# Gate projections of five feed-forward networks as seven block products instead of eight, each network in thirds

## The reference, cut to what matters

```python
def conv_ffn(n, w_up, conv_w, conv_b, w_down):
    u, g = jnp.split(n @ w_up, 2, axis=-1)
    gp = jnp.pad(g, ((0, 0), (pad, pad), (0, 0)))
    gc = sum(gp[:, j:j + S] * conv_w[j] for j in range(CONV_WIDTH)) + conv_b
    return (jax.nn.silu(gc) * u) @ w_down

def swiglu(x, w_gate, w_up, w_down):
    return (jax.nn.silu(x @ w_gate) * (x @ w_up)) @ w_down
```

## Time and profile before

| | us |
|---|---|
| median of 3 runs | 2785.27 (2784.6 to 2785.38) |
| span of the profiled execution | 2783.7 |
| PE busy | 2765.9 (99%) |
| DVE busy | 1427.2 (51%) |
| ACT busy | 1006.1 (36%) |
| POOL busy | 509.2 (18%) |

### The profile page before, as it was taken

The page is one execution under the profiler, slowest core; times in us unless marked ns, Lnnn a source line. Parts: engine busy times, 40 slices in busy tenths (PEclk is TensorE's granted clock), DMA queues, the critical chain, the costliest instruction groups (busy, mean ns, idle before and its releaser), DMA issues.

```text
span 2783.7 us, 33669 instructions
## 1 busy us (share of the span) xinstructions
PE 2765.9 (99%) x12836; PEld 2293.1 (82%) x12836; DVE 1427.2 (51%) x1392; ACT 1006.1 (36%) x1099; POOL 509.2 (18%) x364
## 2 busy tenths in 40 slices
PE   9999999999999999999999999999999999999999
PEld 7978889878888888888778888888888888888887
DVE  5778766566654444343575444334443455644422
ACT  4333633434432344332263444324443222344421
POOL 0124013041101310052123100121110222501100
PEclk9999999999999999999999999999999999999999
DMA  4212024223222322323212222232223322232232
GB/s 165 90 62 79 31 106 148 79 76 106 91 105 95 115 92 90 105 91 105 99 35 74 104 91 97 99 106 104 92 90 106 106 98 99 91 105 91 90 106 91
DMA packets 39676, 264.97 MB, mean 95 GB/s; under 512 B 4528, under 2 KB 5808, under 8 KB 8240
## 3 DMA queue, kind: packets, MB, share of 16 engines
q1 hardware_dynamic: 38016, 259.02, 26.8%
q10 hardware_dynamic: 1584, 4.87, 0.5%
HBM read 261.77 MB, written 2.10 MB: 95 GB/s over the span
## 4 chain that ended last, share of the span: by engine, by line
PE 96%; DVE 2%; ACT 1%; issue 0%; DMA 0%; SPq 0%; POOL 0%; DVEq 0%; POOLq 0%; ACTq 0%
PE ps L1793 30%; PE ps L1794 30%; PE ps L1795 30%; PE ps L1956 1%; PE ps L2022 1%; PE ps L2053 1%; PE ps L2347 1%; PE ps L2319 1%; PE ps L1978 1%; DVE w_lo L901 0%; PE ps L2036 0%; PE ps L2331 0%; ACT w_hi L450 0%; DMA stage<-in_stream 0%; PE ps L1833 0%
## 5 line engine op out<-in xcount | busy, mean ns | idle before, releaser
L450 ACT ACTIVATE w_hi<-stage 128x2048 fp32r<-128x2048 f32 x241 | 462.8, 1920 | 1354.3 <-PE ps L1795 1351.8
L1793 PE MATMUL ps<-x_hi,w_hi 128*128 128x512 f32 x2400 | 943.3, 393 | 2.2 <-DVE w_lo L977 2.0
L1795 PE MATMUL ps<-x_hi,w_lo 128*128 128x512 f32 x2400 | 934.0, 389 | 0.0
L1794 PE MATMUL ps<-x_lo,w_hi 128*128 128x512 f32 x2400 | 933.9, 389 | 0.0
L901 DVE TENSOR_TENSOR w_lo<-stage,w_hi 128x2048 fp32r<-128x2048 f32 x241 | 602.1, 2498 | 397.1 <-ACT w_hi L450 397.1
L1793 PEld LDWEIGHTS ps<-x_hi,w_hi 128*128 128x128 f32 x2400 | 450.6, 188 | 98.9 <-issue 3.5
L1794 PEld LDWEIGHTS ps<-x_lo,w_hi 128*128 128x128 f32 x2400 | 450.7, 188 | 95.4 <-issue 3.4
L1795 PEld LDWEIGHTS ps<-x_hi,w_lo 128*128 128x128 f32 x2400 | 450.5, 188 | 93.9
L1793 PE MATMUL ps<-f_hi,w_hi 128*128 128x512 f32 x880 | 342.7, 389 | 0.0
L1794 PE MATMUL ps<-f_lo,w_hi 128*128 128x512 f32 x880 | 342.3, 389 | 0.0
L1795 PE MATMUL ps<-f_hi,w_lo 128*128 128x512 f32 x880 | 342.3, 389 | 0.0
(11 more groups left out here) (401 smaller groups left out, 2616.3 us busy)
## 6 DMA issues: line engine op xcount, KB each, us to landing
stage<-in_stream SPq DMA_DIRECT2D x242, 1024.0 KB, 4.9
...
```

The costliest lines, as they stand in the source:

```text
L450: act.activation(w_hi[slot][:, :], stage[slot][:, :], ACT.Copy).then_inc(hi_ready, 1)
L1793: pe.matmul(out_ap, wh, xh, start=first, stop=False)
L1794: pe.matmul(out_ap, wh, xl, start=False, stop=False)
L1795: return pe.matmul(out_ap, wl, xh, start=False, stop=last)
```

## The change

Of a gate chunk's matrix A (1024 rows of input by 256 output columns) and the tokens B (1024 by 512), both are cut into halves each way: A into 512x128 blocks, B into 512x256. Eight block products make the two gate tiles; with sums of blocks on both sides seven do (Strassen's method, in the variant with 4 sums of weights and 4 of tokens). Each product is 4 row tiles, 3 matmuls each, of 256 columns.

- Rounds with seven products: 4 to 10 of FFN 0, 2 to 10 of the others (`SEVEN_FROM`). The rest stay at eight.
- DVE makes the four sums of weights from `stage` (`gate_sums`), ACT rounds them (`s_hi`), DVE subtracts (`s_lo`). Only three of the four blocks are also used singly, so the chunk's own split is 1536 wide.
- Once an FFN, ACT scales one quarter of `h` (`t_half`), DVE makes the four sums of tokens (`token_sums`, 16 instructions), ACT rounds and DVE subtracts (`token_lo`).
- DVE puts the products together: five steps while the chunk runs (`gate_early`; ACT first copies product 1 out of PSUM), two after it, and then two multiplications by `rstd` in SBUF (`gate_evac`).
- Each FFN is three parts of 4, 4 and 3 rounds, each followed by its share of down: four chunks, one for each pair of output tiles, of 8, 8 or 6 row tiles. The number of chunks stays 34 an FFN. DVE adds a share to `h` three times. `f_hi` and `f_lo` hold 8 tiles instead of 22, which frees the room for the sums.
- In FFN 1, `stat(3)`, its root and its reciprocal move to round 1, POOL's rescaling of `h` to rounds 1 to 3, and the first share of down waits for it.
- The FFNs are no loops any more: each step is written out on every engine.

Several semaphores were merged under new names elsewhere, with the same waits. The core of the diff:

```diff
+HALF = S // 2
+KP = KT // 2
+PARTS = [("a", 0, 4), ("b", 4, 4), ("c", 8, 3)]
+SEVEN_FROM = [4, 2, 2, 2, 2]
+NONE_OF = FT // 2
...
+f_hi = place("f_hi", HID, [P, 8, S], F32R)
+f_lo = place("f_lo", hid(8), [P, 8, S], F32R)
...
+s_hi = place("s_hi", hid(32), [P, 4 * KP * P], F32R)
+s_lo = place("s_lo", hid(36), [P, 4 * KP * P], F32R)
+s_f = place("s_f", hid(40), [P, 4 * KP * P])
+snap = place("snap", ROPE, [P, 3, HALF])
...
+S1, S3, S2, S4 = range(4)
+T1, T2, T3, T4 = range(4)
+SNAP_1, U2, U3 = range(3)
+PRODUCT = {1: (4, 0), 2: (4, 1), 6: (5, 0), 7: (6, 0), 5: (7, 0)}
+QUARTER = {(0, 0): 0, (1, 0): 1, (1, 1): 2, (0, 1): 3}
...
+T_GROUPS = {i: {0: [0, 1], 1: [2, 3]} if i == 0 else {0: [0, 1, 2, 3]} for i in range(5)}
+T_ROUND_AT = {i: 1 if i == 0 else 0 for i in range(5)}
...
+def gate_hi(i, it):
+    c, _ = gate_chunk(i, it)
+    if not seven(i, it):
+        return split_hi((c, 0))
+    split_hi((c, 0), SINGLES)
+    act.wait_ge(s_sum, 4 * nth(i, it) + 4)
+    act.activation(s_hi[:, :], s_f[:, :], ACT.Copy).then_inc(s_rounded, 1)
+def first_product(n):
+    act.wait_ge(seven_done, 4 * n + 1)
+    act.activation(snap[:, SNAP_1, :], seven_at(1), ACT.Copy).then_inc(seven_snap, 1)
+def t_half(i):
+    for j in range(KP):
+        act.activation(t_f[:, T3, j, :], h[:, j, HALF:S], ACT.Copy, scale=pc(GAIN[i], j)).then_inc(t_scaled, 1)
...
+def ffn(i):
...
+    for part, base, count in PARTS:
+        end = base + count
+        for it in range(base, end):
+            c, t = gate_chunk(i, it)
+            if i == 1 and it == 1:
+                stat(NS0["renorm"])
+            if it + 1 < end:
+                gate_hi(i, it + 1)
             else:
+                split_hi((c + 2, 0))
...
+            split_hi((c + 3, 0))
+            if it == T_ROUND_AT[i]:
+                act.wait_ge(t_sum, 16 * (i + 1))
+                for q in range(4):
+                    act.activation(t_hi[:, q, :, :], t_f[:, q, :, :], ACT.Copy).then_inc(t_rounded, 1)
+            if it + 1 < end and seven(i, it + 1):
+                first_product(nth(i, it + 1))
+            rounded(it, 0)
+            rounded(it, 1)
+        if part != "c":
+            c = C0[_down_name(i, part)]
+            for j in range(4):
+                if j == 2:
+                    gate_hi(i, end)
+                else:
+                    split_hi((c + j + 2, 0))
+            if seven(i, end):
+                first_product(nth(i, end))
...
+def gate_lo(i, it):
+    c, _ = gate_chunk(i, it)
...
+    split_lo((c, 0), SINGLES)
+    dve.wait_ge(s_rounded, nth(i, it) + 1)
+    dve.tensor_tensor(s_lo[:, :], s_f[:, :], s_hi[:, :].bitcast(F32), ALU.subtract).then_inc(s_ready, 1)
+def gate_sums(i, it):
+    c, _ = gate_chunk(i, it)
+    n, w = nth(i, it), KP * P
+    a11, a12, a22, a21 = (stage[c % 2][:, w * q:w * q + w] for q in range(4))
+    s1, s3, s2, s4 = (s_f[:, w * q:w * q + w] for q in range(4))
+    dve.wait_ge(landed[c % 2], 16 * (c // 2 + c % 2))
...
+    dve.tensor_tensor(s1, a21, a22, ALU.add).then_inc(s_sum, 1)
+    dve.tensor_tensor(s3, a11, a21, ALU.subtract).then_inc(s_sum, 1)
+    dve.wait_ge(s_sum, 4 * n + 1)
+    dve.tensor_tensor(s2, s1, a11, ALU.subtract).then_inc(s_sum, 1)
+    dve.wait_ge(s_sum, 4 * n + 3)
+    dve.tensor_tensor(s4, s2, a12, ALU.subtract).then_inc(s_sum, 1)
+def gate_early(i, it):
+    n = nth(i, it)
+    dve.wait_ge(seven_snap, n + 1)
+    dve.tensor_tensor(gate_b[:, 0, LEFT], seven_at(2), snap[:, SNAP_1, :], ALU.add)
+    dve.wait_ge(seven_done, 4 * n + 2)
+    dve.tensor_tensor(snap[:, U2, :], seven_at(6), snap[:, SNAP_1, :], ALU.add).then_inc(seven_sum, 1)
+    dve.wait_ge(seven_done, 4 * n + 3)
+    dve.wait_ge(seven_sum, 5 * n + 1)
+    dve.tensor_tensor(snap[:, U3, :], seven_at(7), snap[:, U2, :], ALU.add).then_inc(seven_sum, 1)
+    dve.wait_ge(seven_done, 4 * n + 4)
+    dve.tensor_tensor(gate_b[:, 0, RIGHT], snap[:, U2, :], seven_at(5), ALU.subtract).then_inc(seven_sum, 1)
+    dve.wait_ge(seven_sum, 5 * n + 2)
+    dve.tensor_tensor(gate_b[:, 1, RIGHT], snap[:, U3, :], seven_at(5), ALU.subtract)
+def gate_evac(i, it):
+    c, t = gate_chunk(i, it)
+    dve.wait_ge(chunk_done, c + 1)
...
+    n = nth(i, it)
+    dve.tensor_tensor(gate_b[:, 1, LEFT], seven_at(4, t), snap[:, U3, :], ALU.add).then_inc(seven_sum, 1)
+    dve.wait_ge(seven_sum, 5 * n + 3)
+    dve.tensor_tensor(gate_b[:, 0, RIGHT], gate_b[:, 0, RIGHT], seven_at(3, t), ALU.subtract).then_inc(seven_sum, 1)
+    for e in range(2):
+        dve.wait_ge(seven_sum, 5 * n + 4 if e else 5 * n + 5)
+        dve.tensor_tensor(gate_b[:, e, 1:1 + S], gate_b[:, e, 1:1 + S], rstd[:, :], ALU.mult).then_inc(acc_evac, 1)
+def token_sums(i, j):
+    done, gain = 16 * i + 4 * j, (pc(GAIN[i], j), pc(GAIN[i], KP + j))
+    b11, b21, b22 = h[:, j, 0:HALF], h[:, KP + j, 0:HALF], h[:, KP + j, HALF:S]
+    dve.wait_ge(t_scaled, 4 * i + j + 1)
+    dve.scalar_tensor_tensor(t_f[:, T1, j, :], b11, gain[0], t_f[:, T3, j, :], ALU.mult, ALU.subtract).then_inc(t_sum, 1)
+    dve.scalar_tensor_tensor(t_f[:, T3, j, :], b22, gain[1], t_f[:, T3, j, :], ALU.mult, ALU.subtract).then_inc(t_sum, 1)
+    dve.wait_ge(t_sum, done + 1)
+    dve.scalar_tensor_tensor(t_f[:, T2, j, :], b22, gain[1], t_f[:, T1, j, :], ALU.mult, ALU.add).then_inc(t_sum, 1)
+    dve.wait_ge(t_sum, done + 3)
+    dve.scalar_tensor_tensor(t_f[:, T4, j, :], b21, gain[1], t_f[:, T2, j, :], ALU.mult, ALU.subtract).then_inc(t_sum, 1)
+def token_lo(i, q):
+    dve.wait_ge(t_rounded, 4 * i + q + 1)
+    dve.tensor_tensor(t_lo[:, q, :, :], t_f[:, q, :, :], t_hi[:, q, :, :].bitcast(F32), ALU.subtract).then_inc(t_ready, 1)
...
+scale = SCALE[f"down{i}"]
+for part, base, count in PARTS:
+    end = base + count
+    for it in range(base, end):
+        c, t = gate_chunk(i, it)
+        gate_evac(i, it)
+        if it + 1 < end:
+            gate_lo(i, it + 1)
+        else:
+            split_lo((c + 2, 0))
+        dve.wait_ge(f_ready, past(FT * i + 2 * it))
...
+        for j in T_GROUPS[i].get(it, []):
+            token_sums(i, j)
+        if it == T_ROUND_AT[i] + 1:
+            token_lo(i, 2)
+            token_lo(i, 3)
+        dve.wait_ge(chunk_done, c + 2)
...
+        split_lo((c + 3, 0))
+        if it + 2 < end and seven(i, it + 2):
+            gate_sums(i, it + 2)
+        if it == T_ROUND_AT[i]:
+            token_lo(i, 0)
+            token_lo(i, 1)
...
+        if it + 1 < end and seven(i, it + 1):
+            gate_early(i, it + 1)
+        if i == 1 and it == 1:
+            dve.wait_ge(std_ready, NS0["renorm"] + 1)
+            dve.reciprocal(sq[:, :], ssum[:, :]).then_inc(rstd_ready, 1)
+    if part != "c":
+        c, t = C0[_down_name(i, part)], T0[_down_name(i, part)]
+        for j in range(4):
+            dve.wait_ge(chunk_done, c + j + 1)
+            for e in range(2):
+                m = 2 * j + e
+                if i == 1 and part == "a":
+                    dve.wait_ge(renormed, KT + m + 1)
+                dve.scalar_tensor_tensor(h[:, m, :], ps[:, (t + m) % 4, :], scale, h[:, m, :], ALU.mult, ALU.add).then_inc(acc_evac, 1)
+            if j == 2:
+                gate_lo(i, end)
+            else:
+                split_lo((c + j + 2, 0))
+            if j == 1 and seven(i, end):
+                gate_sums(i, end)
+            if j == 3 and seven(i, end + 1):
+                gate_sums(i, end + 1)
+        if seven(i, end):
+            gate_early(i, end)
...
+if i == 1 and it == 1:
+    pool.wait_ge(t_sum, 16 * (i + 1))
+    for m in range(KT):
+        pool.tensor_scalar(h[:, m, :], h[:, m, :], pc("final_norm", m), None, ALU.mult).then_inc(renormed, 1)
+    pool.wait_ge(rstd_ready, NS0["renorm"] + 1)
+if i == 1 and it in (2, 3):
+    for m in range(KP * (it - 2), KP * (it - 1)):
+        pool.wait_ge(renormed, KT + m)
+        pool.tensor_tensor(h[:, m, :], h[:, m, :], sq[:, :], ALU.mult).then_inc(renormed, 1)
...
+def eight(c, t, ready):
+    begin(c, t, 2)
...
+    mm.then_inc(chunk_done, 1)
+def seven_products(i, it):
+    c, t = gate_chunk(i, it)
+    n = nth(i, it)
+    def single(k, m):
+        return lambda j: w_at(c, quarter(KP * k, m) + j * P, P)
+    def summed(q):
+        return lambda j: (s_hi[:, (KP * q + j) * P:(KP * q + j + 1) * P], s_lo[:, (KP * q + j) * P:(KP * q + j + 1) * P])
+    def tokens(k, half):
+        at = slice(HALF * half, HALF * half + HALF)
+        return lambda j: (x_hi[:, KP * k + j, at], x_lo[:, KP * k + j, at])
+    def token_sum(q):
+        return lambda j: (t_hi[:, q, j, :], t_lo[:, q, j, :])
+    def product(p, w, b):
+        for j in range(KP):
+            mm = products(seven_at(p, t), w(j), b(j), j == 0, j == KP - 1)
+        return mm
+    begin(c, t, 2)
+    product(1, single(0, 0), tokens(0, 0))
+    product(2, single(1, 0), tokens(1, 0)).then_inc(seven_done, 1)
+    pe.wait_ge(s_ready, n + 1)
+    pe.wait_ge(t_ready, 4 * (i + 1))
+    product(6, summed(S2), token_sum(T2)).then_inc(seven_done, 1)
```

(70 more changed lines are left out.)

325 lines of the change are left out of this document (143 added, 182 removed).

## The result

| | before | after |
|---|---|---|
| median of the runs, us | 2784.99 | 2759.08 (2758.39 to 2760.73, 4 runs) |
| ratio to before, 95% interval | | 0.9907 (0.9894 to 0.9919) |
| span of the profiled execution, us | 2783.7 | 2757.0 |
| PE matmuls | 12836 | 14384 |
| DVE busy, us | 1427 | 1828 |

Faster by 25.9 us, which is the predicted change to a tenth.

What follows compares the result with a forecast made beforehand. TensorE (PE), busy 99% of the span, was taken as the bound. The terms -34.4 + 3 + 1 + 4 + 0.5 = -25.9 us took 2785.3 to 2759 us, range 2749 to 2780.

Steps and rivals of the forecast that it cites:

- TensorE's saving: In 43 gate chunks, 84 matmuls of 256 columns replace 48 of 512: 0.80 us less each, 34.4 us gained.
- DVE in a seven-product round: In steady gate rounds of FFNs 1 to 4, DVE needs 17.7 of 20.96 us and fits: cost 0.
- First down chunk of the last third: In each FFN's last down share, PE waits for `f_lo` at row tile 4: cost 3 us (0 to 6).
- Starts of FFNs 1 to 4: Token sums delay DVE at FFN starts, leaving no spare time: cost 1 us (0 to 6), for FFNs 2 to 4.
- FFN 1: At its start, with the middle norm, POOL and DVE block each other: cost 4 us (0 to 9).
- End of down 0: After FFN 0's down, POOL's sum for `both()` ends about 3 us later relative to PE: cost 0.5 us (0 to 5).
- Nothing is late: Rival for the whole kernel: all waits come to nothing, 2751 us; chance 0.18.
- Unrolled code starves PE: Rival in the FFNs: straight code's 80 to 150 more packets cost 40 to 75 us, 2790 to 2825; chance 0.05.
- DVE becomes the bound: Rival in every seven-product round: DVE takes 25.0 us, total 2844; slower once a round passes 23.6 us; chance 0.05.

Runs made afterwards that it cites:

- eight products in halves: Kernel after without sums; in the 43 chunks each 512-column product done as two of 256, 96 matmuls for 48: 2821.27 us, ratio 1.0131.
- the kernel with 8 products: Kernel after with all gate chunks as eight products, its thirds, unrolled code and new orders kept: 2793.11 us, ratio 1.0029.
- two subtractions more: Kernel after, with the subtraction that makes `s_lo` done two extra times for every seven-product chunk: 2786.05 us, ratio 1.0004.
- one more: Kernel after, with the subtraction that makes `s_lo` done one extra time for every seven-product chunk: 2759.87 us, ratio 0.9911.
- both edits: Kernel after, with POOL's additions for `both()` put ahead after down 0, and `f_lo` written before the weight split in last thirds' last rounds: 2750.61 us.
- `f_lo` first: Kernel after, with DVE writing `f_lo` before a later chunk's weight split in the last third's last round: 2755.47 us, ratio 0.9896.

## Why the prediction was right, step by step

**TensorE's saving, 34.4 us: right.** Starts 0.120 us apart (the chunk by itself: eight products in halves), 34.0 us between the kernels with and without seven products, 34.3 with both waits removed. The Trainium skill's figures (page "TensorE: Matmul & The Clock Gate", section "Back-to-back issue gap") would have made the halves 96 x 262 against 48 x 518 cycles at 2.4 GHz, 0.12 us a chunk and 5 us in all; measured were 28.

**DVE in a seven-product round: right for the bound, too high by 1.8.** Predicted 17.7 us with its waits on own results, near 16 of them busy; measured 15.75 busy and 5.06 idle, so 15.9 taken. FFN 0's round shows 19.45 busy, 20 predicted. The 1.5 us for ten waits on own results were most of the error. Only three of them are for the result just ahead (L1028, L1039, L1059), and each starts 0.11 to 0.19 us later than it would without, some 0.4 us a round; the others cost nothing. The 0.15 us of idle time that I had read off the loops of before is about 0.04 in straight code. The first two of the convolution's three instructions in the kernel with 8 products, 0.04 us between the end of one and the start of the next (before, the second had 3.3 us of idle time ahead of its 22 in the earlier trace rows):

```profile
664.27 0.54 DVE L1126 TENSOR_SCALAR up_b<-gate_b,par 128x512 f32<-128x512 f32 x1
664.85 0.75 DVE L1128 SCALAR_TENSOR_TENSOR up_b<-gate_b,par,up_b 128x512 f32<-128x512 f32 x1
```

At 19.45 us busy FFN 0's rounds build no lag; the prediction's 22.5 (its own terms add up to 22.2) was too high.

I was also wrong on ACT: 10.7 us a round predicted, 7.67 measured, less than the 8.84 of before in spite of the sums' rounding. ACT in the same rounds, before and after:

```profile
1602.21 1.92 ACT L450 ACTIVATE w_hi<-stage 128x2048 fp32r<-128x2048 f32 x1 [5.90 <-PE ps L1795]
1604.15 1.28 ACT L493 ACT_TABLE_LOAD   x1
...
1616.79 1.28 ACT L450 ACT_TABLE_LOAD   x1
```

```profile
1678.23 1.49 ACT L508 ACTIVATE w_hi<-stage 128x1536 fp32r<-128x1536 f32 x1 [5.84 <-PE ps L1997]
1679.62 1.91 ACT L517 ACTIVATE s_hi<-s_f 128x2048 fp32r<-128x2048 f32 x1
1681.43 1.14 ACT L579 ACTIVATE gate_b<-gate_b 128x512 f32<-128x512 f32 x2
```

The loop had loaded a table before its silu and another before its copies, 2.57 us in every round. The straight code has neither, nor has the straight code with 8 products. That also takes a table load out of ACT's part in the chains at the starts and in FFN 1; how much of their spare time it makes was not measured.

**First down chunk of the last third, 3 us: right.** 3.5 in the trace, 3.6 when it is taken out. FFN 0 had no lag of its own, 0.65 us where I had 1.0; the others 0.73 where I had 0.5. The waits themselves are 0.4 to 0.5 us, and the matmul after each also starts late.

**Starts of FFNs 1 to 4, 1 us: wrong by 1 us, and by more in its reasoning.** I had "Nothing is left over". FFN 1's token sums and last token rests after down 0, and the matmul that is first to use the latter, in the kernel after:

```profile
982.20 0.48 DVE L1066 SCALAR_TENSOR_TENSOR t_f<-h,par,t_f 128x256 f32<-128x256 f32 x1
...
982.99 0.48 DVE L1069 SCALAR_TENSOR_TENSOR t_f<-h,par,t_f 128x256 f32<-128x256 f32 x1
983.50 0.48 DVE L1071 SCALAR_TENSOR_TENSOR t_f<-h,par,t_f 128x256 f32<-128x256 f32 x1
...
989.03 1.28 DVE L1140 TENSOR_TENSOR up_b<-ps,rstd 128x512 f32<-128x512 f32 x2
...
1005.00 2.35 DVE L1076 TENSOR_TENSOR t_lo<-t_f,t_hi 128x1024 fp32r<-128x1024 f32 x2
...
1012.31 0.28 PE L1996 MATMUL ps<-t_lo,s_hi 128*128 128x256 f32 x1
```

The 16 sums take 6.8 us (982.20 to 989.03) where I had 8.4. Here the error is the length: I had added up 16 x 0.48, but they start 0.40 us apart (982.20 to 982.99 is two steps), and only the fourth of each group, which waits for the third's result, starts 0.51 after it. The rests end at 1007.3 and PE uses them 5 us later; some of this is that PE itself lost 4.7 us at `both()`. In FFNs 2 to 4 the spare time is 2.6: two subtractions more (4.6 us) gave a stop of 1.97 us at each, one more (2.3 us) gave none.

**FFN 1, 4 us: wrong, it cost 0.** POOL and DVE do meet, but it is POOL that pays. Its first pass of the middle norm, to be held against the earlier trace rows:

```profile
1012.56 19.29 POOL L1877 TENSOR_SCALAR h<-h,par 128x512 f32<-128x512 f32 x8
```

2.4 us each in place of 1.57. DVE lost about 4 us to it up to gate 3's weights (`f_lo` 3.29 us for two in place of 1.28) and 2.2 more in round 3's `f_lo` (3.49), but the room that I had put at nothing was larger, by the shorter token sums and waits on DVE and, as far as ACT is in that chain, the table loads gone. PE's stop in `both()` gave room too, but was not needed: with both edits PE does not stop there, and there is still no wait in FFN 1. It takes two subtractions more to fill that room, and then this is the longest stop of all, 4.49 us: the right place, the wrong amount.

**End of down 0, 0.5 us: wrong, 4.7.** The failed step is "POOL needs 9.2 us a pair ... so it ends about 3 us later". The 9.2 are the time of a pair when pairs came 29.9 us apart. At 8.16 us apart DVE's `w_lo` and `x_lo` passes run beside more of POOL's work, and the first three pairs took 11.1, 10.9 and 10.3: the sum came 13.7 us after the last down chunk (959.46 to 973.14), 6.6 later than before and not 3, and PE wanted it after 10.9. I had the contention in the text ("with more contention 7 or more") and put it at nothing in the sum. A stop of 3.1 us then has a price that I had not thought of, 1.6 us at half clock after it. Taking the stop away gave what the trace said: 4.6 us by itself, 4.9 on top of `f_lo` first. That it is DVE that slows POOL is read from the times of the instructions; no edit took DVE's work away there.

The sum of what the traces show is -34.4 + 3.5 + 4.7 = -26.2 us; predicted were -25.9, with 4 + 1 us too much and 4.2 + 0.5 too little. The saving and the last thirds were right in their mechanism; that the other three terms' errors, of 4 to 5 us each way, came out at nothing is luck.

**The rivals.** *Nothing is late* (2751): not this kernel, but it is what both edits give, 2750.6. *Unrolled code starves PE*: the code did grow, 113 packets for 56, and "issue" at the main line is 8.5 us over 23 places for 8.3 before. 57 packets more cost nothing, and the 0.5 us a packet at which I had priced this rival stand in no row of either kernel. *DVE becomes the bound*: not here, and its turning point was wrong. I gave 23.6 us a round; with two subtractions more the kernel is level with the one before at 20.24 us busy, where rounds still fit, through the starts, FFN 1, FFN 0 and the clock.
